# Two gate projections moved from the last neighbourhood pair to the second and third differential head

## The chip, the cores and the metric

The kernel runs on one core of one Trainium2 chip. The metric is the device time of one execution in microseconds (us); lower is better.

## The reference

Two layers of a diffusion trunk act on 1024 latent tokens and 128 context tokens (1152 rows of 1024 channels). In each layer:

```
gate, (na_q, na_k, na_v, na_z, f_u, f_z, d_q, d_k, d_v, d_z, g) = mixer_input(x, c, norm_g[l], w_mod[l], b_mod[l], w_in[l])
o_na = neighbourhood_attention(...)      # 8 heads x 64; softmax over a window of the grid plus the context keys
o_f  = fourier_mix(f_u, fnet_w[l])
o_d  = diff_attention(...)               # 4 heads, two softmax maps each, 128 values
g = sigmoid(gate_logits)                 # 3 x 1024 channels: the gates that this case is about
y = sum_b g_b * ((outs[b] * silu(zs[b])) @ w_branch_l[b])
x = x + gate * (y @ w_out_l)
```

The 3 x 1024 gate channels come from the same input `h` as the queries, keys and values. They are needed only in the merge at the end of the layer, so their projections may be computed anywhere before it. All products are exact to about fp32: each operand is split into a high and a low half, and three products are added.

## The kernel before, in words

**Chunks and units.** A projection of 128 channels is a *chunk*: a weight block of 1024 x 128 (512 KB). A chunk is computed in three *units* of 384 tokens (`NC = 3`, `CH = 384`), and a unit is 24 matmuls of 384 columns on TensorE (8 blocks of channels x 3 products, `unit`, L730). Chunk kinds are `q`, `k`, `v`, `z` and `g`; there are 24 gate chunks `g` to a layer, numbered 0 to 23.

**Order of the work.** One layer is: four neighbourhood pairs (phase `na`, p = 0 to 3, two heads each), the Fourier branch (`fn`), four differential heads (`df`, h = 0 to 3), the merge and the output projection. Attention leaves TensorE waiting on softmax, so projections are laid between its steps. `fillers(l, ph, p)` is the table written by hand: for each pair and head, a string of chunk kinds and the number `at` of its first gate. `plan()` makes the order of all weight blocks from it.

**Steps of a pair.** Attention goes over nine query tiles (`TILES = 9`: eight latent tiles and a context tile), one step each. `na_steps` deals the pair's units to them: two units in the first steps, one in the rest, so that all are used. A step on TensorE is: the transposes of the probabilities of tile t (L888), the scores of tile t+1 (L769), in layer 0 a small *modulation* product (L779, `modulation`), the first unit, the fold of the modulation (L785), the values of tile t (L900), and a second unit if there is one. On VectorE and ScalarE the softmax of tile t+1 runs meanwhile (L1673, L1291, L1684), then the product with the z gate (L1701).

**Modulation.** While layer 0 runs its pairs, it computes 32 blocks of modulation weights for later use, eight to a pair (`MOD_STEPS = 8`), in steps t = 0 to 7. Each needs its own 512 KB weight block in `mraw`, of which there is one buffer. SyncE issues load i in `mod_to` (L530) once block i-1 has been used (`mr_used`); `modulation(i)` on TensorE waits for the landing (`mr_load`).

**SyncE's queue.** SyncE issues all transfers in program order. For each filler chunk c, number j of its pair: `weights_to` (weights two chunks ahead, L494), then `mod_to` up to a count that a tuple gives for j, then `keep_streaming(c)`, which for a gate waits until ScalarE has evacuated the chunk's last unit (L1152) and stores the gate to `gates_dram` (L517, 576 KB). In the last pair, after chunk j = 0, six loads of Fourier tables follow (L584 to L587, some 2.3 MB), and only then chunk j = 1 has its turn. The core of it:

```
for j, c in enumerate(fillers(l, "na", p)):
    weights_to(CHUNK[c] + 3)
    if l + 1 < DEPTH:
        mod_to(MOD_STEPS * p + (3, 4, 6, 7, 8)[j])
    keep_streaming(c)
    if p == HEADS - 1 and j == 0:
        ...
```

**Steps of a differential head.** `df_steps` takes one unit before the first step and deals the rest: one to a step, two in the steps that `DF_TWO` lists by the number of units left. `df_banks` gives the PSUM banks that follow from it. A step is: transposes (L1032), the scores of the next tile (L769), a unit cut into three parts between the transposes, perhaps a second unit, and in every other step the values (L1041). A head opens with the transposes of its values (L755) and, from h = 1 on, with sums of squares of the head before (L999). `GATES_NA` is the number of gates that are computed in the pairs; it chooses buffers and store counts for the gates.

Of the kernel before, what the change touches and what calls it, by code (L numbers as in the profile page):

```python
# [29 lines left out]
HEADS = 4  # L30
# [13 lines left out]
MOD_STEPS = LATE_MODS // HEADS  # L44


def fillers(l, ph, p):

    kinds = {"na": ("qkgvg", "qkgvg", "qkgvg", "ggggg"), "df": ("qgkgvg", "qkgvg", "qkgvg", "gggggg")}[ph][p]
    at = {"na": (0, 2, 4, 6), "df": (11, 14, 16, 18)}[ph][p]  # L50
    out = []
    for kind in kinds:
        if kind == "g":
            out.append(("g", l, "", at))
            at += 1
        else:
            out.append((kind, l, ph, p + 1))
    return out


def plan():

    out = []
    for l in range(DEPTH):
        for ph in ("na", "fn", "df"):
            if ph == "fn":
                out += [(r, l, ph, m) for r in "uzw" for m in range(HEADS)]
                continue
            out += [(r, l, ph, 0) for r in "qkv"]
            for p in range(HEADS):  # L70
                out += [("z", l, ph, p)] + fillers(l, ph, p)
        out += [("b", l, "", i) for i in range(3 * KT)]
        out += [("o", l, "", m) for m in range(KT)]
    return out
# [29 lines left out]
def gate_no(c):  # L104

    return c[1] * 3 * KT + c[3]


def na_steps(l, p):

    units = [(c, n) for c in fillers(l, "na", p) for n in range(NC)]
    more, steps = len(units) - TILES, []
    for t in range(TILES):
        steps.append([units.pop(0) for _ in range(2 if t < more else 1)])
    return steps


GATES_NA = 11
DF_TWO = {17: (0, 1, 2, 3, 4, 5, 6, 7), 14: (0, 1, 2, 4, 6)}


def df_steps(l, h):

    units = [(c, n) for c in fillers(l, "df", h) for n in range(NC)]
    steps = [[units.pop(0)]]
    two = DF_TWO[len(units)]
    for t in range(TILES):
        steps.append([units.pop(0) for _ in range(2 if t in two else 1)])
    return steps
# [77 lines left out]
def late_mod(i):  # L207

    return (0, 2 * KT + i) if i < KT else (1, i - KT)


def build(nc, x_in, cache_na_k, cache_na_v, cache_diff_k, cache_diff_v, cvec, norm_g, w_mod,
# [188 lines left out]
    def by_chunk(ap):  # L401
        return ap.rearrange("p (c n) -> p c n", n=CH)
# [27 lines left out]
    def unit_evac(c, n):  # L430

        if c[0] == "z":
            return S.z_evac, NC * ZGATE_NO[c] + n + 1
        return S.u_evac, NC * PLAIN_NO[c] + n + 1
# [44 lines left out]
    with nc.Block() as block:  # L479
# [3 lines left out]
        def _(sp):  # L483
# [3 lines left out]
            def weights_to(n_end):  # L487

                while issued[0] < min(n_end, len(STREAM)):
                    n = issued[0]  # L490
                    if n >= 2:
                        sp.wait_ge(S.w_lo, n - 1)
                    c = STREAM[n]
                    sp.dma_start(wraw[:, n % 2, 0:chunk_k(c), :], weight(*c)).then_inc(w_load[n % 2], 16)  # L494
                    issued[0] += 1
# [14 lines left out]
            def keep_streaming(c):  # L510

                weights_to(CHUNK[c] + 3)
                kind, l, ph, p = c
                if kind == "g":
                    sp.wait_ge(*unit_evac(c, NC - 1))
                    src = na_gates[p % 2] if p < GATES_NA else gst
                    sp.dma_start(gates_dram[p], src[:]).then_inc(S.g_store, 16)  # L517
                if kind in "kv":
                    out = {"na": (new_na_k, new_na_v), "df": (new_diff_k, new_diff_v)}[ph]["kv".index(kind)]
                    src = kraw[:, TL + PAST:] if kind == "k" else vT[:, TL:]  # L520
                    sp.wait_ge(*unit_evac(c, NC - 1))
                    sp.dma_start(out[l, p], src).then_inc(S.k_store, 16)

            def mod_to(n_end):

                while mods[0] < n_end:
                    i = mods[0]
                    if i:
                        sp.wait_ge(S.mr_used, i)
                    sp.dma_start(mraw[:], w_mod[late_mod(i)]).then_inc(S.mr_load, 16)  # L530
                    mods[0] += 1

            def cached(l, ph, p, n):

                ck, cv = {"na": (cache_na_k, cache_na_v), "df": (cache_diff_k, cache_diff_v)}[ph]
                if p:
                    sp.wait_ge(S.x_split, 2 * n)
                sp.dma_start(kraw[:, TL:TL + PAST], ck[l, p]).then_inc(S.kc_load, 16)
                if p:
                    sp.wait_ge(S.vc_lo, n)  # L540
                sp.dma_start(vraw[:], cv[l, p]).then_inc(S.vc_load, 16)
# [12 lines left out]
            for l in range(DEPTH):  # L554
# [9 lines left out]
                for p in range(HEADS):  # L564
                    n, u = 2 * HEADS * l + p, l * HEADS + p
                    weights_to(CHUNK["z", l, "na", p] + 3)
                    if p + 1 < HEADS:
                        cached(l, "na", p + 1, n + 1)
                        if p:
                            sp.wait_ge(S.na_b, u * 2 * TILES)  # L570
                        sp.dma_start(bias[:, (p + 1) % 2], rpb[l, p + 1]).then_inc(S.bias_load, 16)
                    for j, c in enumerate(fillers(l, "na", p)):
                        weights_to(CHUNK[c] + 3)
                        if l + 1 < DEPTH:
                            mod_to(MOD_STEPS * p + (3, 4, 6, 7, 8)[j])
                        keep_streaming(c)
                        if p == HEADS - 1 and j == 0:

                            sp.wait_ge(S.x_split, 2 * (n + 1))
                            sp.wait_ge(S.v_done, 3 * (n + 1))  # L580
                            sp.wait_ge(S.vc_lo, n + 1)
                            sp.wait_ge(S.k_store, 32 * (n + 1))
                            sp.wait_ge(S.na_b, u * 2 * TILES)
                            sp.dma_start(tab_c[:], dft_c).then_inc(S.tab_load, 16)  # L584
                            sp.dma_start(tab_x[:], dft_x).then_inc(S.tab_load, 16)
                            for i in range(4):
                                sp.dma_start(tab_t[i][:], dft_t[:, i]).then_inc(S.tab_load, 16)  # L587

                    sp.wait_ge(S.na_o, TILES * (u + 1))
                    sp.dma_start(outs_dram[0, p], obuf[:]).then_inc(S.o_store, 16)  # L590
# [522 lines left out]
        def _(act):  # L1113
# [22 lines left out]
            def evacuate(c, n):  # L1136
# [7 lines left out]
                elif kind == "g":  # L1144
                    if n == 0:
                        at = gate_no(c)
                        if p >= GATES_NA:
                            act.wait_ge(S.g_store, 16 * at)
                        elif p >= 2:
                            act.wait_ge(S.g_store, 16 * (at - 1))  # L1150
                    to = na_gates[p % 2] if p < GATES_NA else gst
                    fn(to[:, cols], src, ACT.Tanh, scale=0.5).then_inc(S.u_evac, 1)  # L1152
# [103 lines left out]
            for l in range(DEPTH):  # L1256
# [111 lines left out]
                def fn_gate(m):  # L1368

                    g = projected("z", l, "fn", m)  # L1370
                    if m == 0:
                        act.wait_ge(S.o_store, 16 * (2 * HEADS * l + HEADS))
                        act.wait_ge(S.g_store, 16 * (l * 3 * KT + GATES_NA))
                    fn(by_chunk(fzs[m][:]), g, ACT.Tanh, scale=0.5).then_inc(S.th_ready, 1)
# [148 lines left out]
        def _(dve):  # L1523
# [84 lines left out]
            for l in range(DEPTH):  # L1608
# [38 lines left out]
                def silu_unit(c, n):  # L1647

                    _, _, ph, p = c
                    to = (df_zs[p % 2] if ph == "df" else zs)[:, n * CH:(n + 1) * CH]  # L1650
                    dve.wait_ge(S.z_tanh, NC * ZGATE_NO[c] + n + 1)
                    v.scalar_tensor_tensor(out=to, in0=to, scalar=1.0, in1=ps[:, BANK[c, n], 0:CH],
                                           op0=ALU.add, op1=ALU.mult).then_inc(S.z_evac, 1)
# [485 lines left out]
```

## Time and profile before

| | |
|---|---|
| time, median of 3 runs | 2940.73 us (2940.59 to 2941.97) |
| time of the profiled execution | 2940.5 us |
| its span, first to last instruction | 2938.6 us |
| TensorE busy | 2877.4 us, 98% |
| VectorE, ScalarE, GpSimd busy | 1330.6, 1076.5, 614.0 us |
| mean granted TensorE clock | 0.996 of full speed |

The span is what the trace covers; the execution's own time is 1.9 us longer. Busy times are of one engine each and overlap. Consecutive matmuls overlap too, so the time of a piece of TensorE's work is read from where it begins to where the next piece begins.

### The profile page before, as it was taken

The page shows a single profiled execution, that of the slowest core. Times are in us where ns is not written, and L with a number is a line of the kernel's source. Part 1 is how long each engine was busy: PE and PEld are TensorE (multiplying, and loading weights), DVE is VectorE, ACT ScalarE, POOL GpSimd, SP SyncE. Part 2 cuts the span into 40 slices and gives each one's busy share as a digit, 9 for nine tenths or more (in the row PEclk, how much of TensorE's full clock was granted, in tenths as well). Part 3 has the DMA queues.
Part 4 walks back from the last instruction along what each step waited for, and adds up shares of the span by engine and source line. Part 5 has one row for each costly group of instructions (what it writes and reads, how often), then busy time and mean ns, then how long its engine had stood idle before and what let it go on. Part 6 is the DMA issues. An engine that isn't in the chain of part 4 may idle for free.

```text
span 2938.6 us, 44082 instructions
## 1 busy us (share of the span) xinstructions
PE 2877.4 (98%) x18396; PEld 2756.4 (94%) x18396; DVE 1330.6 (45%) x2291; ACT 1076.5 (37%) x1947; POOL 614.0 (21%) x312
## 2 busy tenths in 40 slices
PE   6999999999999999999999999999999999999998
PEld 5999999999999999999999999999999989899997
DVE  4343443123557575446344434421146567554543
ACT  4333333221444544422343333323133444443231
POOL 0221221122221212122431221211221121211242
PEclk9999999999999999999999999999999999999999
DMA  5332224102111102254421121220211111215532
GB/s 224 102 110 82 102 90 137 67 15 78 42 47 47 48 32 94 80 203 141 133 79 65 66 82 39 94 83 22 70 41 45 44 48 47 78 51 183 165 110 94
DMA packets 84278, 248.55 MB, mean 85 GB/s; under 512 B 9201, under 2 KB 30193, under 8 KB 83057
## 3 DMA queue, kind: packets, MB, share of 16 engines
q1 hardware_dynamic: 84080, 245.74, 24.5%
q8 instruction: 146, 2.39, 0.3%
q14 instruction: 52, 0.42, 0.0%
HBM read 191.71 MB, written 54.00 MB: 84 GB/s over the span
## 4 chain that ended last, share of the span: by engine, by line
PE 89%; DVE 5%; ACT 2%; DMA 2%; issue 1%; SPq 1%; DVEq 0%; POOL 0%; POOLq 0%; ACTq 0%
PE ps L730 44%; PE ps L713 18%; PE ps L823 6%; PE ps L769 6%; PE ps L900 3%; PE ps L1041 3%; PE ps L1032 2%; PE ps L961 2%; PE ps L888 2%; PE ps L943 1%; DVE e L1839 1%; DVE stat L1822 1%; ACT e L1435 1%; DMA wmod<-w_mod 1%; DVE aTl L1846 1%
## 5 line engine op out<-in xcount | busy, mean ns | idle before, releaser
L730 PE MATMUL ps<-hhi,whi 128*128 128x384 f32 x2640 | 916.3, 347 | 5.7 <-DVE obuf L1854 3.3
L730 PE MATMUL ps<-hhi,wlo 128*128 128x384 f32 x2640 | 886.3, 336 | 0.0
L730 PE MATMUL ps<-hlo,whi 128*128 128x384 f32 x2640 | 884.1, 335 | 0.0
L1956 POOL TENSOR_TENSOR wlo<-wraw,whi 128x1024 fp32r<-128x1024 f32 (+1 forms) x188 | 415.8, 2212 | 2063.6 <-ACT whi L1127 2063.5
L730 PEld LDWEIGHTS ps<-hhi,whi 128*128 128x128 f32 x2640 | 500.0, 189 | 24.1 <-issue 7.3
L730 PEld LDWEIGHTS ps<-hlo,whi 128*128 128x128 f32 x2640 | 497.1, 188 | 0.9
L730 PEld LDWEIGHTS ps<-hhi,wlo 128*128 128x128 f32 x2640 | 495.9, 188 | 0.0
L1127 ACT ACTIVATE whi<-wraw 128x1024 fp32r<-128x1024 f32 (+1 forms) x188 | 174.5, 928 | 229.9 <-PE ps L713 209.3
L1444 ACT ACTIVATE aTh<-ps 128x512 fp32r<-128x512 f32 (+1 forms) x200 | 96.5, 482 | 278.4 <-PE ps L1032 278.4
L1691 DVE TENSOR_TENSOR ptl<-ps,pth 128x512 fp32r<-128x512 f32 (+1 forms) x144 | 82.1, 611 | 246.8 <-ACT pth L1301 246.6
L1822 DVE TENSOR_REDUCE stat<-ps 128x1 f32<-128x1152 f32 x144 | 176.5, 1231 | 16.9 <-PE ps L769 16.0
L1435 ACT ACTIVATE e<-ps,stat 128x1152 f32<-128x1152 f32 x144 | 162.3, 1128 | 55.9 <-DVE stat L1822 55.9
L1152 ACT ACTIVATE gst<-ps 128x384 f32<-128x384 f32 x144 | 70.5, 490 | 265.3 <-PE ps L730 265.3
L1846 DVE TENSOR_TENSOR aTl<-ps,aTh 128x512 fp32r<-128x512 f32 (+1 forms) x200 | 108.3, 541 | 106.8 <-ACT aTh L1444 106.0
L1291 ACT ACTIVATE sn<-sn,stat 128x512 f32<-128x512 f32 (+1 forms) x144 | 95.9, 666 | 112.5 <-DVE stat L1676 106.6
L713 PE MATMUL ps<-omh,whi 128*128 128x384 f32 x576 | 132.6, 338 | 0.7 <-POOL wlo L1956 0.7
L713 PE MATMUL ps<-omh,wlo 128*128 128x384 f32 x576 | 131.6, 336 | 0.0
L713 PE MATMUL ps<-oml,whi 128*128 128x384 f32 x576 | 131.6, 336 | 0.0
L769 PE MATMUL ps<-kh,qh 64*128 64x128 f32 (+3 forms) x656 | 117.1, 353 | 0.0
L1032 PE MATMUL ps<-ident,e 128*128 128x128 f32 x584 | 100.5, 279 | 11.4 <-DVE aTl L1846 8.8
L769 PE MATMUL ps<-kl,qh 64*128 64x128 f32 (+3 forms) x656 | 109.4, 329 | 0.0
L769 PE MATMUL ps<-kh,ql 64*128 64x128 f32 (+3 forms) x656 | 109.0, 328 | 0.0
(199 smaller groups left out, 4835.8 us busy)
## 6 DMA issues: line engine op xcount, KB each, us to landing
wraw<-w_in SPq DMA_DIRECT2D x128, 512.0 KB, 4.2
gates_dram<-gst SPq DMA_DIRECT2D x48, 576.0 KB, 3.0
gth<-gates_dram SPq DMA_DIRECT2D x48, 576.0 KB, 4.9
mraw<-w_mod SPq DMA_DIRECT2D x32, 512.0 KB, 3.8
wraw<-w_branch SPq DMA_DIRECT2D x48, 256.0 KB, 2.8
bias<-rpb SPq DMA_DIRECT2D x8, 1280.0 KB, 6.0
outs_dram<-obuf SPq DMA_DIRECT2D x16, 576.0 KB, 3.9
oraw<-outs_dram SPq DMA_DIRECT2D x16, 576.0 KB, 3.8
```

Source lines behind the costliest of these rows:

```text
L713: x = mm(ps[:, at + n, 0:CH], a[:, s % 2, k, :], b[k][:, n * CH:(n + 1) * CH], start=(k == 0 and a is whi and b is mhi), stop=(k == kt - 1 ...
L730: x = mm(ps[:, bank, 0:CH], a[:, s % 2, k, :], b[:, k, n * CH:(n + 1) * CH], start=(k == 0 and a is whi and b is hhi), stop=(k == KT - 1 a ...
L769: x = mm(out, a[r, t * P:(t + 1) * P], b[r, k0:k1], start=(i == 0), stop=(i == 2))
L823: x = mm(ps[:, bank, 0:CH], a[:, k, :], b[:, k, n * CH:(n + 1) * CH], start=(k == 0 and a is hi and b is hhi), stop=(k == KT - 1 and a is lo))
L1032: x = nc.tensor.transpose(ps[:, DF_TURN_BANK[h][t], j * P:(j + 1) * P], e1[:, t % 2, kt * P:(kt + 1) * P], ident[:])
L1127: fn(halves(s)[0][:, 0:kt, :], wraw[:, n % 2, 0:kt, :], ACT.Copy).then_inc(S.w_hi, 1)
L1291: fn(sn[:, e, 0:nk], sn[:, e, 0:nk], ACT.Exp, bias=stat[:, e, 1:2], accum_out=stat[:, e, 3:4]).then_inc(S.na_e, 1)
L1435: fn(out, flat[:, 1536 * m:1536 * m + nk], ACT.Exp, bias=stat[:, t % 2, m:m + 1], accum_out=stat[:, t % 2, 2 + m:3 + m]).then_inc(S.df_e, 1)
L1444: fn(aTh[:, 4 * g:4 * g + w, (t % 2) * P:(t % 2 + 1) * P], ps[:, DF_TURN_BANK[h][t], 0:w * P].rearrange("p (t n) -> p t n", n=P), ACT.Copy ...
L1822: v.tensor_reduce(stat[:, t % 2, m:m + 1], flat[:, 1536 * m:1536 * m + nk], AX.X, ALU.max, negate=True).then_inc(S.df_m, 1)
L1846: v.tensor_tensor(aTl[at], ps[:, DF_TURN_BANK[h][t], 0:w * P].rearrange("p (t n) -> p t n", n=P), aTh[at].bitcast(F32), ALU.subtract).then ...
L1956: g_.tensor_tensor(lo[:, 0:kt, :], wraw[:, n % 2, 0:kt, :], hi[:, 0:kt, :].bitcast(F32), ALU.subtract).then_inc(S.w_lo, 1)
```

## The change

The last pair of the `na` phase computes three gates where it computed five. The second and third differential heads compute three where they computed two, in the order `qgkgvg` that the first head has. The tables that hang on this follow: first gate numbers, `GATES_NA`, `DF_TWO`, and the tuple for `mod_to` in the last pair.

```diff
 def fillers(l, ph, p):
 
-    kinds = {"na": ("qkgvg", "qkgvg", "qkgvg", "ggggg"), "df": ("qgkgvg", "qkgvg", "qkgvg", "gggggg")}[ph][p]
-    at = {"na": (0, 2, 4, 6), "df": (11, 14, 16, 18)}[ph][p]
+    kinds = {"na": ("qkgvg", "qkgvg", "qkgvg", "ggg"), "df": ("qgkgvg", "qgkgvg", "qgkgvg", "gggggg")}[ph][p]
+    at = {"na": (0, 2, 4, 6), "df": (9, 12, 15, 18)}[ph][p]
...
-GATES_NA = 11
-DF_TWO = {17: (0, 1, 2, 3, 4, 5, 6, 7), 14: (0, 1, 2, 4, 6)}
+GATES_NA = 9
+DF_TWO = {17: (0, 1, 2, 3, 4, 5, 6, 7)}
...
                     for j, c in enumerate(fillers(l, "na", p)):
                         weights_to(CHUNK[c] + 3)
                         if l + 1 < DEPTH:
-                            mod_to(MOD_STEPS * p + (3, 4, 6, 7, 8)[j])
+                            mod_to(MOD_STEPS * p + ((3, 4, 6, 7, 8) if p + 1 < HEADS else (3, 6, 8))[j])
                         keep_streaming(c)
```

## Rows read from the trace of the kernel before

**Rows 1.** The page, part 1: busy time, share and instructions.

```profile
PE 2877.4 (98%) x18396; PEld 2756.4 (94%) x18396; DVE 1330.6 (45%) x2291; ACT 1076.5 (37%) x1947; POOL 614.0 (21%) x312
```

**Rows 2.** TensorE's waits: us in total, times, longest.

```profile
PE ps L1032 <- DVE aTl L1846: 8.8, 11, 0.9
...
PE ps L1032 <- DVE e L1839: 2.2, 8, 0.3
```

**Rows 3.** Differential heads 2, 4, 1: length; PE, PEld, DVE, ACT, POOL busy; clock; DMA.

```profile
865.61:986.63 121.02, 118.20 (x783) 110.03 (x783) 79.02 (x93) 55.91 (x100) 24.24 (x10) 1.00 0.13 44
...
1107.66:1238.66 131.00, 130.27 (x855) 122.47 (x855) 66.77 (x85) 57.88 (x103) 19.92 (x9) 1.00 0.21 75
736.64:865.61 128.97, 127.93 (x848) 121.35 (x847) 70.88 (x90) 53.13 (x98) 27.43 (x11) 1.00 0.13 41
```

**Rows 4.** Chain, last pair of layer 0: start, us, what.

```profile
439.56 4.17 PE ps L730 x24
443.72 0.87 PE ps L888 x8
444.60 1.01 PE ps L769 x12
...
450.56 0.12 PE ps L785 x2
...
452.19 4.17 PE ps L730 x24
456.36 0.87 PE ps L888 x8
```

**Rows 5.** Chain, last pair of layer 1.

```profile
1924.25 0.87 PE ps L888 x8
...
1930.49 1.41 PE ps L900 x12
```

**Rows 6.** Timeline of VectorE in that stretch: start, us, instruction.

```profile
1929.53 0.49 DVE L1684 TENSOR_SCALAR sn<-sn,stat 128x512 f32<-128x512 f32 x1
```

**Rows 7.** Timeline of SyncE's issues, last pair of layer 0.

```profile
451.11 0.33 SPq L517 DMA_DIRECT2D gates_dram<-gst  x1
...
453.31 1.86 SPq L587 DMA_DIRECT2D tab_t<-dft_t  x4
455.21 1.12 SPq L494 DMA_DIRECT2D wraw<-w_in  x1
458.88 0.33 SPq L530 DMA_DIRECT2D mraw<-w_mod  x1
```

**Rows 8.** From issue to landing: the mraw load issued at 458.88.

```profile
DMA to landing us min/median/max: 6.6/6.6/6.6
```

**Rows 9.** The same for the mraw load issued at 484.16, with nothing ahead.

```profile
DMA to landing us min/median/max: 3.5/3.5/3.5
```

**Rows 10.** Chain, seventh step of the same pair.

```profile
506.92 0.87 PE ps L888 x8
507.80 0.72 PE ps L769 x6
```

**Rows 11.** Timeline of SyncE's issues beside it.

```profile
507.48 0.33 SPq L517 DMA_DIRECT2D gates_dram<-gst  x1
507.85 0.43 SPq L494 DMA_DIRECT2D wraw<-w_in  x1
509.15 0.33 SPq L530 DMA_DIRECT2D mraw<-w_mod  x1
```

**Rows 12.** From issue to landing: the mraw load issued at 509.15.

```profile
DMA to landing us min/median/max: 5.0/5.0/5.0
```

**Rows 13.** Stretches at the start of layer 1, columns as in rows 3.

```profile
1523.50:1526.03 2.53, 0.09 (x1) 0.00 (x0) 0.00 (x0) 1.14 (x4) 2.34 (x1) 1.00 0.53 206
1526.03:1529.50 3.47, 3.47 (x11) 3.47 (x12) 0.00 (x0) 2.85 (x3) 2.86 (x2) 0.51 0.44 151
```

**Rows 14.** Chain, the unit right after that wait.

```profile
1526.03 5.99 PE ps L730 x24
```

## The prediction

> **What bounds the kernel now.** I read the page's busy times first: TensorE is busy 98% of the span, no other engine half of it [rows 1]. So the change can only win TensorE's idle time, and only lose by making new. Next the list of TensorE's waits: apart from the kernel's start, the largest groups are transposes of a differential head (L1032) that wait on VectorE, 8.8 and 2.2 us [rows 2]. Then the heads' stretches show where. The second head, with fifteen units, is idle for 121.02 - 118.20 = 2.8 us; the fourth, with eighteen, for 0.7 us [rows 3]. The third head, and both again in layer 1, repeat the second within 0.02 us: four such heads. Last the chain through the last pair: TensorE's pieces follow each other without a gap [rows 4, 5]. Nothing is won by taking work away there but the work itself.
>
> **The work that moves.** A second unit of a pair's step takes 4.17 us [rows 4]. The pair had 15 units and gets 9, one to a step: minus 6 x 4.17 = 25.0 us in each layer, minus 50.0 us in all.
> The second and third head get the eighteen units of the fourth. That one takes 131.00 us with them [rows 3]. The first takes 128.97 but lacks the 1.64 us of square sums and a little of its prologue, and so says the same within some tenths. Hence 131.00 - 121.02 = 10.0 us for three more units that cost 3 x 4.17 = 12.5 us by themselves; the other 2.5 us is idle time filled. Over four heads plus 39.9 us. The first head has the same string of chunks, a two-unit step in each of the first eight and the same rope work on VectorE, so its store waits, its k chunk and its rope parts stand as a model for the new heads: I add nothing for them. Sum so far: -50.0 + 39.9 = **-10.1 us**.
>
> **The softmax under one unit.** In layer 1 a step without the second unit lasts from 1924.25 to the end of the values, 1931.90, 7.65 us [rows 5]. VectorE ends the probabilities of the next tile at 1930.02 [rows 6], 5.8 us after the step's start, and they are wanted at 7.65. That leaves 1.8 us, so nothing waits. Layer 0 has the modulation in the step too, so more room. The steps t = 6 and 7 already run with one unit and show no gap. Cost nothing; the cover is TensorE's unit and values.
>
> **The modulation loads of layer 0.** Here a wait is added. SyncE's order is: for j = 0, loads up to block 26, then the wait for the first gate's evacuation, its store, six tables; for j = 1, weights, then block 27. Before, the first gate's three units were used up by the first unit of step 1 (450.56), and the store left at 451.11 [rows 4, 7]. Now its third unit is in step 2. Block 27 is wanted in step 3. So its load, which had more than a step of lead, has none.
> When it is wanted: step 1 begins at 439.56, where the second unit stood. A step with four key tiles and one unit lasts 456.36 - 443.72 - 4.17 = 8.47 us [rows 4]. Step 3 begins at 439.56 + 2 x 8.47 = 456.50 and its modulation could start after transposes and scores, 0.87 + 1.01 us later, at 458.4.
> When it lands: the gate's last unit ends 450.56 - 443.72 = 6.84 us into a step, so at 448.03 + 6.84 = 454.87, and the store follows 0.55 us later, at 455.42. In the trace, from the store's issue to the landing of the mraw load behind the tables are 458.88 + 6.6 - 451.11 = 14.4 us [rows 7, 8]. There mraw was issued 2.5 us after SyncE was free, but its landing was set by the transfers ahead of it, since alone it takes 3.5 us [rows 9]. So it lands at 469.8: TensorE waits **11.4 us**. Behind it stand the unit, the values and all that follows; no other engine has work to catch up. Bounds: if the load took only 3.5 us from its earliest issue (455.21 + 1.12 + 4.31 = 460.6), it would wait 5.7 us; if crowding adds a further transfer's time, some 12.5. I take 11.4, since that row has the very same transfers ahead.
> The second place is the tuple's next entry. Blocks 28 and 29 have their loads in time. Block 30 is loaded after the second gate's evacuation, in step 5, and wanted in step 6. After the unit's end come the fold and the values, 452.19 - 450.56 = 1.63 [rows 4], then transposes and scores of step 6, 0.87 + 0.72 [rows 10]: 3.2 us. The store leaves 0.55 us after the unit's end, and mraw lands 509.15 + 5.0 - 507.48 = 6.7 us after the store [rows 11, 12]. It can now be issued 0.9 us sooner, behind the weight issue, so between 5.8 and 6.7, say 6.3. Wait: 0.55 + 6.3 - 3.2 = **3.6 us** (3.1 to 4.0). Block 31 again is in time. Layer 1 has no modulation, so these waits come once.
>
> The Trainium skill, "DMA: Bandwidth & Descriptors", section "Anatomy of one DMA — SWDGE (gpsimd) path", fits a transfer as about 2.0 us plus its bytes over 436 GB/s (for another issue path). By that, the 4.0 MB from the store to mraw would take 11.2 us, an estimate from that page, against the 14.4 us of the trace; the first wait would be 8.2 us and the total 3.2 us lower than mine.
>
> **TensorE's clock.** After 2.4 us of idle at 1523.6, the granted clock was 0.51 for 3.47 us, that is the level of 1.2 GHz, with the engine busy throughout [rows 13]; a unit took 5.99 us there in place of the 4.17 to 4.36 [rows 14, 4]. Half speed for 3.47 us loses 1.7 us. Both new waits are longer than that idle stretch, so I count 2 x 1.7 = **3.4 us**; from 0 (the clock stays) to 3.6.
>
> **Sum.** -10.1 + 11.4 + 3.6 + 3.4 = **+8.3 us**. The profiled execution took 2940.5 us, 1.9 more than its span and 0.2 less than the median. On the median: 2940.73 + 8.3 = **2949.0 us**.
>
> **The rivals.** A measurement of this kernel can tell about 0.2%, 5.9 us, from no change.
> *Forecast*, both waits near the size above, 2946.7 to 2953: 0.70.
> *The loads are hidden.* Place: `mod_to` in the last pair of layer 0. If block 27 were there when step 3 wants it, only -10.1 is left: **2930.6 us, faster**. For it: nothing on TensorE waited on mraw before. Against: the order of SyncE's issues puts the load behind an evacuation that ends only 3.5 us before the want, and even alone it takes 3.5 us [rows 9]. It decides from a landing before 458.4, which is 3.0 us after the store's issue. 0.07.
> *The waits are short.* The first load lands at its lower bound (5.7 us), the second wait is 3.1, and the clock falls once: -10.1 + 5.7 + 3.1 + 1.7 = +0.4, **2941.1 us, the same**. For it: TensorE has never waited on this queue, so the landing times are those of transfers that nobody needed early. The Trainium skill's fit above leans to this side. 0.15.
> *The heads don't fill their idle time.* If gate evacuations, which share one buffer in the heads, hold the new units, each head grows by the full 12.5 us: +10 over four, **about 2959 us**. The first and fourth head speak against it. 0.04.
> *The softmax is bared.* If one unit covers too little, each of six middle steps in two layers could lose a microsecond: +12, about 2961 us. Against: the 1.8 us of room. 0.04.
> Range: 2943 to 2953 us. Its lower end takes in most of the way to the short waits, its upper end the crowded load. Faster 0.07; the same 0.15; slower 0.70 + 0.04 + 0.04 = 0.78.
>
> **What would show it.** In the profile after: a wait of TensorE at L779 on the DMA mraw<-w_mod, two times, 11.4 and 3.6 us, the first around 458; granted clock near 0.5 for about 3.5 us after each; the last pair of layer 0 shorter by 25.0 - 18.4 = 6.6 us, that of layer 1 by 25.0; the second and third head 131.0 us, their waits at L1032 gone. I am wrong if no such wait is there, if a head is off by more than 1 us, or if layer 1's pair keeps gaps.

## The result, and the profile after

| | before | changed |
|---|---|---|
| median, nine runs each | 2940.84 us | 2948.28 us |
| lowest to highest | 2938.61 to 2943.27 | 2947.14 to 2950.63 |
| ratio, 95% interval | | 1.0026 (1.0016 to 1.0036) |
| profiled execution, time and span | 2940.5, 2938.6 | 2949.1, 2947.2 |

The changed kernel is slower by 4.7 to 10.6 us; the medians differ by 7.4 us, the two traces by 8.6 us, and the forecast was 8.3 us. Where the 8.6 us lie can be read by cutting both traces at the first instruction of each stretch (the first transposes of values, L755, and the first matmul at L713):

| stretch | before | changed | difference |
|---|---|---|---|
| up to the first pair | 86.84 | 87.88 | +1.0 |
| last pair, layer 0 | 110.44 | 103.66 | -6.8 |
| second head, layers 0 and 1 | 121.02, 121.01 | 131.14, 131.05 | +10.1, +10.0 |
| third head, layers 0 and 1 | 121.03, 121.03 | 131.17, 131.12 | +10.1, +10.1 |
| merge and output of layer 0, with the start of layer 1 | 301.53 | 299.74 | -1.8 |
| last pair, layer 1 | 104.00 | 79.01 | -25.0 |
| everything else | | | +0.8 |

The list of TensorE's waits, which answers to [rows 2], now has an entry that was not there, in second place (columns: us in total, times, longest):

```profile
PE ps L832 <- DVE sq L1605: 16.3, 2, 14.8
PE ps L779 <- DMA mraw<-w_mod: 14.6, 2, 9.7
PE ps L747 <- DVE hlo L1619: 6.0, 2, 5.5
PE ps L1032 <- DVE aTl L1846: 4.7, 8, 0.6
```

L779 is the modulation product, and it waits for its weight block. In the heads, the waits at L1032 on aTl fell from 8.8 to 4.7 us, and those on e are gone from the list. One wait at L1032, of 0.6 us, is left in each of the second and third heads; the first head has the same one in both kernels.

The stretches of the second and third head and of the two last pairs answer to [rows 3] (columns as there):

```profile
859.90:991.04 131.14, 130.10 (x855) 122.89 (x855) 75.35 (x93) 58.25 (x104) 25.59 (x11) 1.00 0.15 49
991.04:1122.22 131.18, 130.14 (x856) 123.09 (x855) 75.36 (x93) 58.27 (x104) 25.58 (x11) 1.00 0.14 49
418.04:521.70 103.66, 88.84 (x695) 83.99 (x693) 44.33 (x141) 35.28 (x84) 10.14 (x6) 0.93 0.31 107
1863.91:1942.92 79.01, 78.78 (x551) 76.09 (x549) 42.44 (x133) 33.74 (x76) 10.17 (x6) 1.00 0.25 88
```

The two last pairs in the kernel before:

```profile
417.00:527.43 110.43, 110.20 (x838) 105.69 (x836) 44.33 (x141) 39.45 (x92) 15.02 (x8) 1.00 0.35 121
1851.02:1955.02 104.00, 103.77 (x695) 100.85 (x693) 42.45 (x133) 38.15 (x84) 14.99 (x8) 1.00 0.25 88
```

A head of eighteen units leaves TensorE idle for 1.0 us, where one of fifteen left 2.8 us [rows 3]. In layer 1 the pair with one unit to a step leaves it idle for 0.2 us, as the pair before did in both layers. In layer 0 it is idle for 14.8 us, and the mean granted clock is 0.93.

SyncE's issues in that pair answer to [rows 7] and [rows 11]:

```profile
456.45 0.33 SPq L517 DMA_DIRECT2D gates_dram<-gst  x1
456.97 0.33 SPq L584 DMA_DIRECT2D tab_c<-dft_c  x1
457.34 0.83 SPq L585 DMA_DIRECT2D tab_x<-dft_x  x1
458.21 1.90 SPq L587 DMA_DIRECT2D tab_t<-dft_t  x4
460.15 0.74 SPq L494 DMA_DIRECT2D wraw<-w_in  x1
460.94 19.76 SPq L530 DMA_DIRECT2D mraw<-w_mod  x3
493.71 0.33 SPq L517 DMA_DIRECT2D gates_dram<-gst  x1
494.08 0.43 SPq L494 DMA_DIRECT2D wraw<-w_in  x1
494.55 8.19 SPq L530 DMA_DIRECT2D mraw<-w_mod  x2
```

And the chain that ended last, in the same stretch. Where [rows 4] had TensorE alone, it now runs through SyncE and a DMA:

```profile
456.45 0.33 SPq L517
...
460.94 8.15 DMA mraw<-w_mod
469.09 0.04 issue
469.13 1.08 PE ps L779 x16
470.21 6.00 PE ps L730 x24
...
493.71 0.33 SPq L517
...
494.55 6.67 DMA mraw<-w_mod
501.23 0.04 issue
501.27 1.08 PE ps L779 x16
```

Read it from the top: gate store, tables, weights, then mraw, which lands at 469.09; TensorE had been ready since 459.4. (The row of three loads at 460.94 merges those of blocks 27 to 29; only block 27 is waited for.) The unit behind it takes 6.00 us in place of 4.36. The second wait is the same without the tables. Windows of this kernel show the clock beside it:

```profile
463.47:469.13 5.66, 0.00 (x0) 0.00 (x0) 0.00 (x0) 0.00 (x0) 0.00 (x0) 0.50 0.87 356
469.13:473.71 4.58, 4.58 (x27) 4.16 (x28) 0.00 (x0) 0.28 (x1) 0.00 (x0) 0.50 0.33 114
501.01:504.43 3.42, 3.16 (x23) 2.74 (x24) 0.00 (x0) 0.28 (x1) 0.00 (x0) 0.50 0.26 53
```

The clock fell to its lower level, 1.2 GHz, 4 us into the first wait and near the end of the second. It stayed there while TensorE worked for 4.58 and 3.16 us, which loses half of that: 2.3 and 1.6 us. While TensorE waited in the first row, no other engine of the core worked either.

### The profile page after: what moved, and what is told of

Same layout as the page of the kernel before. It is cut to its first block, busy times and chain, and to the rows that moved or that the text cites. A ratio compares the mean times of both kernels' runs of the same rounds, so it can differ in the third digit from the quotient of the medians.

```text
span 2947.2 us, 44094 instructions
## 1 busy us (share of the span) xinstructions
PE 2877.5 (98%) x18396; PEld 2761.8 (94%) x18396; DVE 1316.7 (45%) x2291; ACT 1077.1 (37%) x1947; POOL 609.7 (21%) x312
## 4 chain that ended last, share of the span: by engine, by line
PE 92%; DMA 2%; DVE 2%; ACT 1%; SPq 1%; issue 1%; DVEq 0%; POOL 0%; POOLq 0%; ACTq 0%
PE ps L730 46%; PE ps L713 18%; PE ps L823 6%; PE ps L769 6%; PE ps L1041 4%; PE ps L900 3%; PE ps L1032 2%; PE ps L961 2%; PE ps L888 2%; PE ps L943 1%; DMA wraw<-w_in 1%; DMA wmod<-w_mod 1%; PE ps L779 1%; PE ps L747 1%; PE ps L755 1%
## 5 line engine op out<-in xcount | busy, mean ns | idle before, releaser
L1822 DVE TENSOR_REDUCE stat<-ps 128x1 f32<-128x1152 f32 x144 | 176.6, 1231 | 13.5 <-PE ps L769 12.6
L713 PE MATMUL ps<-omh,whi 128*128 128x384 f32 x576 | 132.6, 338 | 0.5 <-POOL wlo L1956 0.5
L713 PE MATMUL ps<-omh,wlo 128*128 128x384 f32 x576 | 131.6, 336 | 0.0
L713 PE MATMUL ps<-oml,whi 128*128 128x384 f32 x576 | 131.6, 336 | 0.0
L1032 PE MATMUL ps<-ident,e 128*128 128x128 f32 x584 | 99.9, 278 | 5.0 <-DVE aTl L1846 4.7
```

Of the source, the lines that this page charges most:

```text
L713: x = mm(ps[:, at + n, 0:CH], a[:, s % 2, k, :], b[k][:, n * CH:(n + 1) * CH], start=(k == 0 and a is whi and b is mhi), stop=(k == kt - 1 ...
L1032: x = nc.tensor.transpose(ps[:, DF_TURN_BANK[h][t], j * P:(j + 1) * P], e1[:, t % 2, kt * P:(kt + 1) * P], ident[:])
L1822: v.tensor_reduce(stat[:, t % 2, m:m + 1], flat[:, 1536 * m:1536 * m + nk], AX.X, ALU.max, negate=True).then_inc(S.df_m, 1)
```

## The experiments

All are compared with runs of the kernel before on the same chip (medians 2939.7 to 2939.9 us).

### Loads one step ahead

```diff
-mod_to(MOD_STEPS * p + ((3, 4, 6, 7, 8) if p + 1 < HEADS else (3, 6, 8))[j])
+mod_to(MOD_STEPS * p + ((3, 4, 6, 7, 8) if p + 1 < HEADS else (4, 7, 8))[j])
```

> The changed kernel with the tuple of the last pair (4, 7, 8) in place of (3, 6, 8): blocks 27 and 30 are loaded ahead of the first and second gate's evacuation. Theory (order of SyncE's issues): both waits of the changed kernel, 9.7 and 4.9 us, go, and with them the two stretches at 1.2 GHz. Block 28 now stands behind the tables; its landing, about 469.1, against a want at 467.8 in the times of the changed kernel leaves a wait of 1.3 us at L779. Time 2932 to 2933 us. Rival (collision with the tables, whichever block stands behind them): a wait of about 10 us moves to block 28 and the time stays near 2945 us or above. Rival (one unit to a step costs something of its own in layer 0): the waits at L779 go, but the pair keeps gaps elsewhere and the time stays above 2936 us.

Measured: 2933.20 us, ratio 0.9977 (0.9968 to 0.9986), faster than the kernel before. The waits for blocks 27 and 30 are gone. One wait is left, for block 28, in the list of waits:

```profile
PE ps L779 <- DMA mraw<-w_mod: 2.4, 1, 2.4
```

It is 2.4 us where 1.3 was expected: the block landed 13.75 us after the gate's store, not 12.6. The clock fell behind it for 3.4 us, and the pair took 89.42 us. Two numbers of a tuple turned a slower kernel into a faster one. The rival that moves the whole wait to block 28 is out, and so is the one with a cost of one unit to a step, which would have kept the time above 2936 us.

### Loads two steps ahead

```diff
-... else (3, 6, 8))[j])
+... else (5, 7, 8))[j])
```

> The changed kernel with the tuple (5, 7, 8): block 28 too is loaded ahead of the first gate's store and the tables. Theory: no wait at L779 at all; last pair of layer 0 shorter than before by 25.0 us, heads longer by 4 x 10.1, sum -9.6 us: 2931.2 us. The first gate's store and the tables leave about 3 us later, with nobody waiting for them. Rival (collision with the tables): a wait of several us at block 29. Rival (cost of its own of one unit to a step): above 2935 us with no wait at L779.

Measured: 2930.33 us, ratio 0.9969 (0.9957 to 0.9980). Its chain through the same steps is TensorE alone again:

```profile
456.65 0.87 PE ps L888 x8
457.53 1.01 PE ps L769 x12
458.54 0.57 PE ps L779 x16
459.11 4.38 PE ps L730 x24
```

SyncE's issues show what was given for it: block 28 goes out ahead of the store, which leaves at 459.55, after step 3's modulation, and nobody waits for it.

```profile
450.71 8.79 SPq L530 DMA_DIRECT2D mraw<-w_mod  x2
459.55 0.43 SPq L517 DMA_DIRECT2D gates_dram<-gst  x1
```

The last pair of layer 0 took 85.44 us, 25.0 less than before, and the heads 131.1. The same kernel was run again with the last group below:

> The same kernel as e2_loads_two_steps_ahead, beside the others of this call on the same chip. Theory: -9.6 us against before, ratio 0.9967, twice what one moved gate gives.

Measured: 2931.04 us, ratio 0.9969 (0.9958 to 0.9981). So the moved work is worth some 9 us, and the two waits with their clock turned that into a loss.

### The tables behind the third gate

```diff
-                        if p == HEADS - 1 and j == 0:
+                        if p == HEADS - 1 and j == 2:
```

> The changed kernel, tuple (3, 6, 8) kept, but the six table loads are issued after the third gate's store and not after the first. Theory (order and crowding both count): the first wait becomes like the second, about 4.6 us, since the load still starts after the evacuation but has only the gate's store and one weight block ahead; the second stays 4.9; 2942 to 2943 us. Rival (the tables are all of it): the first wait goes entirely, the second stays, about 2937 us. Rival (only the late issue counts): both waits stay, 9.7 and 4.9 us, 2948 us.

Measured: 2941.03 us, ratio 1.0008 (0.9999 to 1.0017). Two waits at L779 of 3.9 and 4.0 us, in the list:

```profile
PE ps L779 <- DMA mraw<-w_mod: 7.8, 2, 4.0
```

The first is now like the second, as expected, and each is a little shorter than expected: the load landed 463.77 - 456.96 = 6.8 us after the store. The clock fell in the first and just behind the second. Both rivals are out. By the difference of the two runs, 5.8 us of the first wait of 9.7 us were the tables ahead of the load, and 3.9 us its issue after the evacuation. So the late issues, with no table ahead of a load, already cost with the lower clock all that the moved gates give: the time is that of the kernel before.

### The wait alone, with no gate moved

From the kernel before:

```diff
-mod_to(MOD_STEPS * p + (3, 4, 6, 7, 8)[j])
+mod_to(MOD_STEPS * p + ((3, 4, 6, 7, 8) if p + 1 < HEADS else (3, 3, 6, 7, 8))[j])
```

> The kernel before, no gate moved, with the tuple of the last pair (3, 3, 6, 7, 8) in place of (3, 4, 6, 7, 8): block 27 is loaded only after the second gate's evacuation at the end of step 2 and wanted in step 3. Theory: one wait at L779 of 5.4 to 6.2 us plus 1.6 us for the clock, nothing else: 2940.8 + 7.4 = 2948 us. Rival (two units to a step hide it): no change, 2940.8 us. Rival (the clock does not fall or costs nothing at the end): 2946.5 us.

Measured: 2947.58 us, ratio 1.0027 (1.0015 to 1.0038), the same slowdown as that of the change, with fifteen units in the pair. Chain and stretch:

```profile
472.58 5.78 DMA mraw<-w_mod
...
478.41 1.08 PE ps L779 x16
479.49 6.36 PE ps L730 x24
```

```profile
478.41:483.77 5.36, 5.36 (x30) 4.94 (x31) 0.00 (x0) 0.28 (x1) 0.00 (x0) 0.50 0.28 98
```

The wait was 5.3 us. The clock stayed low for 5.36 us of work, a loss of 2.7 us where 1.6 was expected. Together 8.0 us; the pair grew by 118.26 - 110.44 = 7.8 us. A second unit in the step hides nothing, because it stands behind the modulation in TensorE's order.

### One gate moved

```diff
-    kinds = {"na": ("qkgvg", "qkgvg", "qkgvg", "ggggg"), "df": ("qgkgvg", "qkgvg", "qkgvg", "gggggg")}[ph][p]
-    at = {"na": (0, 2, 4, 6), "df": (11, 14, 16, 18)}[ph][p]
+    kinds = {"na": ("qkgvg", "qkgvg", "qkgvg", "gggg"), "df": ("qgkgvg", "qgkgvg", "qkgvg", "gggggg")}[ph][p]
+    at = {"na": (0, 2, 4, 6), "df": (10, 13, 16, 18)}[ph][p]
...
-GATES_NA = 11
+GATES_NA = 10
...
-mod_to(MOD_STEPS * p + (3, 4, 6, 7, 8)[j])
+mod_to(MOD_STEPS * p + ((3, 4, 6, 7, 8) if p + 1 < HEADS else (3, 4, 7, 8))[j])
```

> Half the change without its wait: from the kernel before, one gate (not two) leaves the last pair (gggg) and goes to the second head (qgkgvg); the third head stays qkgvg. The tuple of the last pair is (3, 4, 7, 8), so that every modulation block is asked for at least a step ahead. Theory (TensorE's idle time in a fifteen-unit head is filled, nothing is lost in the pair): last pair shorter by 3 x 4.17 = 12.5 us in both layers, second head longer by 10.1 in both, third head unchanged at 121.0: -4.8 us against the kernel before, a ratio of 0.9984, half of what e2_loads_two_steps_ahead gave. No wait at L779. Rival (the gain of e2 lies in the later start of the tables and stores, not in the heads): no change, ratio 1.0. Rival (a head gains only if its neighbour is filled too): second head longer by 12.5, no change.

Measured: 2937.82 us, ratio 0.9995 (0.9986 to 1.0004): a miss, since 0.9984 lies outside. The time alone can't be told from no change; the stretches decide against the rivals, for they are as expected: last pair 97.94 us in layer 0 and 91.50 in layer 1, 12.5 less in both; second head 131.11 and 131.07; third unchanged at 121.04 and 121.07. But the Fourier branch of layer 0, from its first matmul to the first head, took 211.96 us in place of 209.21. So I ran it again:

> The same kernel as e3_one_gate_moved, because its profile had something beside the pair and the heads: a wait in the Fourier branch (L943 on xdif) of 2.3 us with a stretch at 1.2 GHz behind it, where the kernel before waits 1.1 us. Theory (scatter of a transfer's landing): the wait is back near 1.1 us, the pair and heads are as in e3_one_gate_moved, and the ratio lies between 0.9984 and 0.9995. Rival (one gate moved makes this transfer late): the wait is 2.3 us again with the clock at 1.2 GHz behind it, ratio 0.9995.

Measured: 2938.13 us, ratio 0.9994 (0.9985 to 1.0003). The rival holds: the wait came back in the second execution, 2.4 us after 2.3, and the Fourier branch took 212.10 us. The chain there, and the stretch behind the wait:

```profile
532.23 6.75 DMA wraw<-w_in
...
539.00 1.06 ACT whi L1127
540.05 0.28 ACT xcs L1346
...
540.78 0.34 DVE xdif L1741
...
541.17 2.07 PE ps L943 x4
```

```profile
541.05:544.46 3.41, 3.29 (x9) 2.93 (x10) 1.47 (x5) 0.38 (x1) 1.44 (x1) 0.50 0.28 54
```

ScalarE must split the next weight block before it copies what TensorE's transform waits for. The block's load is issued behind the two rope tables once the first u chunk is done. In this kernel it takes 6.75 us to land, in the kernel before 5.43, and the wait at L943 grows from 1.1 to 2.4 us, enough here for the clock to fall. The same places in the kernel before:

```profile
543.21 5.43 DMA wraw<-w_in
...
550.83 1.13 PE ps L943 x4
```

One thing sets the slow loads apart. Behind the same two rope tables, this load took 5.2 to 5.5 us in sixteen places of the traces (both layers of the kernel before, of the changed kernel and of the five runs above, and layer 1 of both runs with one gate moved). It took 6.6 and 6.75 us in two, layer 0 of both executions of this kernel. In these two alone, the profile's table of DMA queues has a transfer of 16 KB of the kind "instruction" in the same stretch:

```profile
q8 instruction: 1, 0.02, 0.9%
```

And the end of the load looks different. Here are its last 0.9 us in this kernel, then in the kernel before (columns as in [rows 3], the last is GB/s):

```profile
538.10:538.98 0.88, 0.64 (x4) 0.32 (x2) 0.00 (x0) 0.00 (x0) 0.00 (x0) 1.00 0.09 33
547.70:548.64 0.94, 0.94 (x7) 0.89 (x6) 0.00 (x0) 0.00 (x0) 0.00 (x0) 1.00 1.02 418
```

The DMA engines were almost all done, and a small rest kept the load from landing. That the instruction transfer had held this rest up fits, but no run takes it away, so that cause is not shown.

### The Fourier weights ahead of the rope tables

```diff
+                weights_to(CHUNK["u", l, "fn", 3] + 1)
                 sp.wait_ge(*evacuated("u", l, "fn", 0))
                 sp.dma_start(cosT[:], rope[0]).then_inc(S.rope_load, 16)
```

With one gate moved:

> e3_one_gate_moved with one line more: the third and fourth u weight blocks of the Fourier branch are loaded before SyncE waits for the first u chunk and not after the rope tables. Theory: the wait at L943 on xdif (2.3 us there, 1.1 in layer 1 and in the kernel before in both layers) goes in both layers, and what is left is the work moved: -4.8 - 2.2 = -7.0 us against before, ratio 0.9976. Rival (the moved gate gives nothing by itself): -2.2 us, ratio 0.9993.

Measured: 2932.94 us, ratio 0.9976 (0.9967 to 0.9985), and no wait at that place in either layer; the Fourier branch takes 207.83 us in both. That accounts for the miss: the load is now asked for so early that its landing no longer matters. With the line the branch is 1.4 us shorter than in the kernel before in each layer, and 4.1 us shorter than with one gate moved alone in layer 0. The pair and the heads give -4.8 us, the branch -2.7, together -7.5; the ratio says -7.1.

With two gates moved and loads two steps ahead:

> e2_loads_two_steps_ahead with the same line. Theory: 2.2 us less than that one, -11.8 us against before, ratio 0.9960, about 2928.5 us; no wait at L943 on xdif and none at L779. Rival (the rope tables, now behind the weights, come late to the first head): the Fourier stretch is shorter but the first head starts its rope late, no gain over e2.

Measured: 2926.27 us, ratio 0.9956 (0.9944 to 0.9968). This is the fastest version, some 13 us below the kernel before (9 to 16 by the interval). The rope tables, now behind the weights, are not late: they leave 14.9 us after the branch's start, as before, and the first head takes 128.95 us, as before. SyncE's issues there (the added line shifts L592 to L593):

```profile
505.99 2.92 SPq L494 DMA_DIRECT2D wraw<-w_in  x2
520.10 0.33 SPq L593 DMA_DIRECT2D cosT<-rope  x1
```

The line alone, on the kernel before, was not run.

## Why the prediction was right

**The result** lay 0.7 us from the forecast of 2949.0, on the median. The mechanism held, but that closeness is luck: the terms were off by -1.7, +1.3, +0.5 and +0.5 us, which nearly cancel. The traces also hold differences that no term is about, among them +1.0 us before the first pair and -1.8 us at the start of layer 1.

**The work that moves.** Right. -25.0 us in layer 1's pair, as worked out. In the heads 10.1 us each and not 10.0. The waits at L1032 in these heads were to be gone, and 0.6 us is left in each. The sum -10.1 was -9.6 in the traces; the kernel with no wait (two steps ahead) shows it whole, ratio 0.9969, about 9 us.

**The softmax under one unit.** Right: 0.2 us idle in the whole pair of layer 1, and in layer 0 the chain of the two-steps kernel has no gap.

**The modulation loads.** Right in place, order and number. The first wait was over-sized, 9.7 for 11.4. The step that failed was the landing: I took 14.4 us from the store's issue, since "that row has the very same transfers ahead", and it was 469.09 - 456.45 = 12.6. That row is the slowest there is: the same nine transfers took 14.3 us in the kernel before, 13.75 with loads one step ahead, 13.4, 13.0 and 12.9 in the three runs with one gate moved, and 12.6 in the changed kernel. One row was no measure of this term; what makes the difference stays open. In both kernels mraw landed 1.2 to 1.3 us behind the weight block ahead of it, so it was bound by the transfers ahead, as forecast. Those were faster in the changed kernel: the weight block landed 455.21 + 9.0 - 451.11 = 13.1 us after the store in the kernel before, and 460.15 + 7.7 - 456.45 = 11.4 us after it in the changed one. The second was under-sized, 4.9 for 3.6: I let an earlier issue bring it forward to 6.3 us after the store, and it landed 501.23 - 493.71 = 7.5 us after, later than the 6.7 of [rows 11, 12]. In the experiments the same three transfers took 6.8 and 6.6 us (tables behind the third gate) and 6.6 us (no gate moved). So this term too has a scatter of nearly a microsecond from one kernel to the next. By the Trainium skill, "DMA: Bandwidth & Descriptors", section "Anatomy of one DMA — SWDGE (gpsimd) path", the 4.0 MB taken as one transfer would have needed 11.2 us, an estimate; that is 1.4 us below this trace, mine was 1.8 us above.

**The clock.** 3.4 us forecast. The work done at 1.2 GHz gives 2.3 + 1.6 = 3.9 us. The mechanism held; the length at the lower level was not the same each time.

**The rivals.** The hidden loads fell with the first trace; the experiment with the wait alone shows that such a load costs 7 to 8 us by itself. The short waits fell with 14.6 us at L779. The heads do fill their idle time: 10.1 us for 12.5 us of units, in all four. The bared softmax fell with layer 1.

## What to carry to other kernels

When filler work is taken out of a step, everything that was timed by that filler moves: here the queue of SyncE, in which a load stood behind a wait for the filler's end. Ask, for each wait in an in-order issue queue, which step now releases it and which step wants what stands behind it. A move that fills 2.5 us of idle time per head was worth having here only with the loads asked for early: one step ahead gave 7 us, two steps ahead 9 us, and a late load took it all back. A wait of a few microseconds on a busy TensorE cost its own length and 1.6 to 2.8 us more at the lower clock.

## What the runs showed of the hardware

**The clock.** The same wait does not always bring the clock down. At the start of layer 1, TensorE waits 2.44 us for a weight split in every one of the eleven traces. In the kernel before, the granted clock was 0.51 behind it [rows 13]; in the changed kernel it stayed up, with the same wait:

```profile
1540.46 0.44 PE L730 MATMUL ps<-hhi,whi 128*128 128x384 f32 x1 [2.44 <-POOL wlo L1956]
```

```profile
1538.00:1540.46 2.46, 0.02 (x1) 0.00 (x0) 0.00 (x0) 1.18 (x3) 2.34 (x1) 1.00 0.52 203
1540.46:1544.00 3.54, 3.54 (x20) 3.54 (x21) 0.00 (x0) 2.76 (x3) 3.04 (x2) 1.00 0.50 148
```

It fell in six of the eleven traces. A wait of 1.6 us in the output projection of layer 0 brought it down in two of eleven, for 3.4 us each time. Three waits of 2.3 to 2.4 us elsewhere (block 28 with loads one step ahead, and L943 in both executions with one gate moved) brought it down each time. So did all five waits of 3.9 us and longer in the last pair, and TensorE then worked for 3.2 to 5.5 us at the lower level. So 1.7 us and more, here and there, belong to no change of the kernel; the -1.8 us of the merge in layer 0, in the first table, are of this kind.

**Landing times.** They are no constants of a list of transfers. The nine from the gate's store to mraw took 12.6 to 14.3 us in six traces, and the load behind the rope tables, steady within 0.4 us in sixteen places, took over a microsecond longer in the two where a 16 KB transfer of the kind "instruction" fell beside it. A load that was due to land just when it was wanted came late in some of these kernels.
